# A three-stage transformer layer in split float32: the order of its transfers, and where two kinds of derived blocks are made

## The reference

```python
u = x @ w_in                                  # 1024 x 1024, four groups of 256 columns
pooled = trailing mean over 2, 4, 8, 16 tokens   # one window per group
m = (einsum(pooled - u, w_group) * scale) @ w_out
h = layer_norm(ALPHA * x + m)
gate, up = split(h @ w_gu, 2)                 # d_ff = 2816
out = layer_norm(ALPHA * h + (silu(gate) * up) @ w_down)   # meta tokens dropped
```

## Time and profile before

| | before |
|---|---|
| median of three runs | 1836.06 us |
| the profiled execution | 1835.27 us, span 1833.5 us |
| granted clock, mean | 0.968 |
| PE busy | 1692.6 us (92%), 7400 matmuls |
| DVE, ACT, POOL busy | 53%, 32%, 32% |
| DMA | 307.75 MB, mean 168 GB/s |
| PE idle and what ended it | DVE split 41.7 us, ACT acc 31.8 us, DMA nat 11.8 us, DVE acc 10.5 us |

### The profile page before, as it was taken

How to read it: one execution, slowest core, us unless ns; L and a number is a source line. 1 busy time by engine, 2 the same in 40 slices (tenths; PEclk the granted TensorE clock), 3 DMA queues, 4 the chain that set the end, 5 groups by cost and what they waited for, 6 DMA issues and landing times.

```text
span 1833.5 us, 18920 instructions
## 1 busy us (share of the span) xinstructions
PE 1692.6 (92%) x7400; PEld 1390.8 (76%) x7400; DVE 975.0 (53%) x1055; ACT 580.2 (32%) x790; POOL 586.1 (32%) x361
## 2 busy tenths in 40 slices
PE   7997876997789999999986999999999899999997
PEld 5886665876568877788875888888888788888786
DVE  6557447683675333344444554444553444458757
ACT  5232212332433333333343333333332433342220
POOL 0004323043233233343322666566652000142001
PEclk9999898998989999999997999999999999999999
DMA  8434866647625344342244445545458544555532
GB/s 327 179 115 165 284 238 222 243 143 245 247 97 162 103 137 127 116 132 69 92 145 154 151 136 157 180 134 156 131 186 265 186 142 154 186 178 202 192 131 100
DMA packets 189704, 307.75 MB, mean 168 GB/s; under 512 B 7728, under 2 KB 137904, under 8 KB 178096
## 3 DMA queue, kind: packets, MB, share of 16 engines
q1 hardware_dynamic: 189616, 306.55, 49.6%
HBM read 218.96 MB, written 87.56 MB: 167 GB/s over the span
## 4 chain that ended last, share of the span: by engine, by line
PE 69%; DMA 11%; DVE 6%; POOL 6%; issue 4%; SPq 2%; ACT 2%; ACTq 0%; DVEq 0%; POOLq 0%
PE acc L913 35%; PE acc L942 13%; PE turn L913 6%; PE turn L942 5%; PE acc L780 5%; PE acc L764 4%; DMA raw<-fold_dram 2%; POOL dt_t L618 2%; DMA dt_raw<-w_down 2%; DMA raw<-w_in 1%; POOL ss_mix L618 1%; DMA fs<-hf_dram 1%; DVE fa L1364 1%; SPq L375 1%; DVE split L1231 1%
## 5 line engine op out<-in xcount | busy, mean ns | idle before, releaser
L913 PE MATMUL acc<-fa,wf 128*128 128x512 f32 x3168 | 739.9, 394 | 43.7 <-ACT acc L1159 31.8
L913 PEld LDWEIGHTS acc<-fa,wf 128*128 128x128 f32 x3168 | 600.1, 190 | 171.3 <-DVE wf L1370 25.5
L942 PE MATMUL acc<-dw,da 128*128 128x512 f32 x1386 | 317.9, 391 | 7.8 <-DVE da L1437 6.1
L942 PEld LDWEIGHTS acc<-dw,da 128*128 128x128 f32 x1386 | 260.9, 189 | 63.6 <-DVE da L1437 7.0
L1370 DVE TENSOR_TENSOR wf<-wt,wf 128x512 fp32r<-128x512 f32 x132 | 122.4, 929 | 206.0 <-ACT wf L1072 205.8
L1370 DVE TENSOR_TENSOR wf<-wr,wf 128x512 fp32r<-128x512 f32 x176 | 169.9, 973 | 83.1 <-ACT wf L1072 82.6
L780 PE MATMUL acc<-split,act_sb 128*128 128x512 f32 x768 | 185.9, 404 | 27.4 <-DVE split L1231 16.1
L764 PE MATMUL acc<-mov,split 128*128 128x512 f32 x768 | 184.9, 401 | 28.3 <-DVE split L1231 25.6
L780 PEld LDWEIGHTS acc<-split,act_sb 128*128 128x128 f32 x768 | 149.7, 196 | 62.7 <-DVE split L1231 13.5
L764 PEld LDWEIGHTS acc<-mov,split 128*128 128x128 f32 x768 | 147.7, 194 | 61.6 <-issue 26.5
L618 POOL TENSOR_TENSOR wt<-wr,wt 128x512 f32<-128x512 f32 x88 | 127.6, 1450 | 171.1 <-DVE wf L1370 171.0
(11 more groups left out here) (94 smaller groups left out, 1329.4 us busy)
## 6 DMA issues: line engine op xcount, KB each, us to landing
wr<-w_gu SPq DMA_DIRECT2D x44, 1024.0 KB, 5.0
dar<-af_dram SPq DMA_DIRECT2D x56, 704.0 KB, 4.1
af_dram<-g SPq DMA_DIRECT2D x33, 512.0 KB, 3.3
raw<-w_in SPq DMA_DIRECT2D x16, 1024.0 KB, 9.4
raw<-fold_dram SPq DMA_DIRECT2D x16, 1024.0 KB, 9.1
fs<-hf_dram SPq DMA_DIRECT2D x14, 1024.0 KB, 4.9
dt_raw<-w_down SPq DMA_DIRECT2D x11, 1024.0 KB, 7.6
wt_dram<-dt_t SPq DMA_DIRECT2D x11, 1024.0 KB, 5.2
```

The costliest lines, as they stand in the source:

```text
L913: mm = nc.tensor.matmul(dst, wf[:, slot, a, k, :], fa[i][:, v, k, :], start=i < 2 and k == 0 and n3 == 0, stop=k == KC - 1 and n3 == 2, sk ...
L942: mm = nc.tensor.matmul(down_bank(k), da[k % 3][:, v, p, :], dw[:, slot, a, :], start=p == 0 and n3 == 0, stop=p == JF - 1 and n3 == 2)
```

## The change

**T forms.** The steps stand by a list, `TF_AT`: three beside block 0's last chunks, six beside `c_in(1, 2)` to `c_mix(1, 3)`, and two (with a last store) beside `c_in(2, 2)` to `c_mix(2, 0)`. In `mixer_block`, `load_x` now stands ahead of the step. POOL takes three forms ahead of `rstd_of(0)`, six ahead of `rstd_of(1)`.

**Turned h.** Pair 0 is turned in the last chunk of block 2, pairs 1 to 3 in `c_in(3, 0)` to `c_in(3, 2)`. They have their own landing buffer, `nat_mix`. `st_mix` is one buffer instead of two. POOL makes pair 0's sums ahead of `rstd_of(2)`. Pairs 4 to 7 are turned one in three units (5 and 6, 8 and 9, 11 and 12, 14 and 15). ACT's `take_turn` waits for `st_stored` and for `ss_made` of the pair before, no more for the landing of its sums.

**Forms.** `hf_dram` is laid out so that a pair is stored in two DMAs (768 KB and 1 MB) with runs of 2 KB and loaded in runs of 2 KB. `fa[i]` becomes `[P, 2, TT, KC, P]`: the moving operand of a product, 512 columns long, now lies in four pieces of 512 B, 2 KB apart. `fs` has four buffers for the exchange: four forms are loaded at unit 17, and the seven splits are spread over units 21 and 22 (`NEW_FORM_AT`).

**Others.** In block 3, `store_h(2, 1..3)` and `load_z(3)` go behind `load_form(1)`, just ahead of the last chunk's load. The last `store_a` and `store_s` go behind the first `load_da` of the down stage's loop.

```diff
             def store_pair(pi):
-                half, cols = pi // TT, slice(pi % TT * P, pi % TT * P + P)
-                forms = hf_dram[half].rearrange("f p k t -> p f k t")
+                half, j = pi // TT, pi % TT
+                forms = hf_dram[half].rearrange("f j p n -> j p f n")[j]
                 sp.wait_ge(turn_taken, 4 * pi + 4)
-                for f, blk in ((0, 1), (3, 2), (6, 3)):
-                    sp.dma_start(forms[:, f, :, cols], st[:, blk]).then_inc(stored, 16)
+                sp.dma_start(forms[:, 0:3, :], st_of(pi)[:, 1:4].rearrange("p f k t -> p f (k t)")).then_inc(st_stored, 16)
                 sp.wait_ge(ss_made, 4 * pi + 4)
-                for f, blk in ((1, 0), (2, 1), (4, 2), (5, 3)):
-                    sp.dma_start(forms[:, f, :, cols], ss[:, blk]).then_inc(stored, 16)
+                sp.dma_start(forms[:, 3:NP, :], ss_of(pi).rearrange("p f k t -> p f (k t)")).then_inc(ss_stored, 16)
...
+            TF_AT = [(0, 5), (0, 6), (0, 7), (1, 2), (1, 3), (1, 4), (1, 5), (1, 6), (1, 7), (2, 2), (2, 3), (2, 4)]
...
-            load_chunk(c_in(LAST, 0), 0, w_in[0])
-            load_chunk(c_in(LAST, 1), 1, w_in[1])
             load_pair(0)
-            load_chunk(c_in(LAST, 2), 0, w_in[2])
+            for i in range(3):
+                load_chunk(c_in(LAST, i), i % 2, w_in[i])
             load_pair(1)
             store_pair(0)
...
-            for j in range(1, TT):
-                store_h(LAST - 1, j)
-            load_z(LAST)
             load_chunk(c_mix(LAST, 2), 0, fold_dram[2])
             store_pair(3)
             load_form(0)
             load_form(1)
+            for j in range(1, TT):
+                store_h(LAST - 1, j)
+            load_z(LAST)
             load_chunk(c_mix(LAST, 3), 1, fold_dram[3])
...
+        NEW_FORM_AT = [(HALF_UNITS - 1, place) for place in range(3, 7)] + [(HALF_UNITS, place) for place in range(3)]
...
-                if k == 0:
-                    if pi < TT and pi >= 2:
-                        act.wait_ge(pair_stored[pi % 2], 112 * (pi // 2))
-                    elif pi > TT:
-                        act.wait_ge(pair_stored[(pi - 1) % 2], 112 * ((pi - 1) // 2 + 1))
...
+                if k == 0 and pi:
+                    act.wait_ge(st_stored, 16 * pi)
+                    act.wait_ge(ss_made, 4 * pi)
...
-                        mm = nc.tensor.matmul(dst, wf[:, slot, a, k, :], fa[i][:, v, k, :],
+                        mm = nc.tensor.matmul(dst, wf[:, slot, a, k, :], fa[i][:, v, :, k, :],
```

More of the change, by code:

```diff
@@ L1 @@
+import functools
 import math
@@ L268, in st_of, with nat_of, fs_uses, fs_holder @@
         def st_of(pi):
-            return st_mix[pi % 2] if pi < 4 else st_gu
+            return st_mix if pi < 4 else st_gu
+        def nat_of(pi):
+            return nat_mix if pi < 4 else nat
+        HF_OF = (0, 3, 4, 1, 5, 6, 2)
+        FS_SLOT = (0, 1, 0, 1, 0, 1, 0, 0, 1, 2, 3, 0, 1, 2)
+        def fs_uses(q):
+            return FS_SLOT[:q].count(FS_SLOT[q])
+        def fs_holder(q):
+            return max((r for r in range(q) if FS_SLOT[r] == FS_SLOT[q]), default=None)
         def ss_of(pi):
@@ L379, in load_form @@
                 if i == 0:
[L380 to L384, removed]
+                    sp.wait_ge(st_stored, 16 * TT * (half + 1))
+                    sp.wait_ge(ss_stored, 16 * TT * (half + 1))
+                if fs_holder(q) is not None:
+                    sp.wait_ge(fa_lo, fs_holder(q) + 1)
+                sp.dma_start(fs[FS_SLOT[q]].rearrange("p j k t -> p j (k t)"),
+                             hf_dram[half, HF_OF[i]].rearrange("j p n -> p j n")).then_inc(fs_landed[FS_SLOT[q]], 16)
             def load_unit(n):
@@ L770, in hidden, with outward @@
                         between(m)
-            def outward(c, slot, half, k0, kn, first, final, bank_is_free):
+            def outward(c, slot, half, k0, kn, first, final, bank_is_free, between=None):
                 chunk_is_split(c)
@@ L783, in outward @@
                                                   stop=final and k == kn - 1 and n3 == 2)
-                    if final and j < TT - 1:
-                        mm.then_inc(out_done, 1)
-                mm.then_inc(chunk_done, 1)
+                    if j < TT - 1:
+                        if final:
+                            mm.then_inc(out_done, 1)
+                    else:
+                        mm.then_inc(chunk_done, 1)
+                    if between is not None:
+                        between(j)
             def fold_pair_free(q):
@@ L1101, in mixer_block @@
                         x_hi(b + 1, i)
+                        if b == LAST - 1 and i == PAIRS - 1:
+                            for k in range(KC):
+                                take_turn(0, k)
                     elif i == 1:
@@ L1509, in _ @@
                         down_w_lo(v)
-                if n == HALF_UNITS - 1:
-                    for q in range(NP + 3, 2 * NP):
-                        form_lo(q)
             dve.wait_ge(prod_done, NP * UNITS)
```

161 lines of the change are left out of this document (88 added, 73 removed).

## The result

Four runs of the changed kernel gave 1760.46 to 1765.40 us, median 1760.84; the kernel before gave 1835.07 beside them. The ratio is 0.960 (95% interval 0.958 to 0.962). The forecast was 1727 with a range of 1708 to 1758: right in sign, 34 us too low, and the measured time lies 2.8 us above the range. The profiled execution took 1760.91 us, with a span of 1759.1 and a mean granted clock of 0.984 (before 0.968).

A forecast was written before the change was run, and what follows sets the result against it. PE was taken as full at full clock for most of the span, losing time to waits in four places. Gains of 27.5 + 18.7 + 24.2 + 17.7 + 18.8 + 2.5 = 109.4 us off 1835.27 gave 1725.9, forecast 1727, range 1708 to 1758.

The forecast's parts named there:

- what stays of the waits in blocks 1 and 2: Mixer blocks 1 and 2: waits of 6.7 and 1.5 us stay; gains of 27.5 and 18.7 us.
- The first wait of the rest: Block 1: PE waits some 2.2 us for DVE's split of the third chunk, behind the first pooling ending at 157.8.
- Block 3: Mixer block 3, turning pairs 1 to 3: 101.0 us, a gain of 24.2 us.
- The wait for the rows: Block 3: PE's wait of 4.97 us for DVE, whose row adds stood behind the late form 0, goes.
- Pairs 4 to 7: Units 5 to 15: three units per pair and a wait for POOL alone remove all 17.7 us lost.
- The exchange: Units 21 and 22: forms waiting in buffers gain 18.8 us; 4 us of wait for DVE's list stays.
- The down stage's start: Start of down stage: weight block goes out about 2 us earlier, gain 2.5 us (0 to 5).
- The moving operand in four pieces: Products' matmuls: taken to cost nothing, since the pieces are 128 elements long.
- Rival 1: Blocks 1 to 3: the queue still sets the pace, +25 us, 1752; chance 0.18.
- Rival 2: Waits left in the forecast are met by the splits' and loads' spread, some 15 us fewer, 1712; chance 0.12.
- Rival 3: Exchange and units still wait for ACT and DVE: exchange 10 us instead of 4, +15 in all, 1742; chance 0.09.
- Rival 4: Units 0 to 43: the moving operand in pieces slows every product, 1936 at a quarter of a matmul; chance 0.03.

The follow-up runs named there:

- both causes taken out: Changed kernel with x loaded behind the row stores and z, and POOL's sums of T forms 1 to 10 over 8 columns: 1730.98 us, ratio 0.944.
- the short sums: Changed kernel with POOL's sums of T forms 1 to 10 made over 8 of 512 columns, transfers kept: 1739.23 us, ratio 0.949.
- the last kernel: Changed kernel with T forms beside units 5 to 15 and new orders at exchange, down stage, block 3 and unit 0: 1705.44 us, ratio 0.930.

## Why the prediction was right in sign and 34 us off

**The step that failed: what stays of the waits in blocks 1 and 2.** The prediction gave them 94.1 and 90.7 us, as clean blocks plus 6.7 and 1.5 of waits; they took 109.2 and 96.5, 20.9 us more. The clean part was right (87.4 and 89.2 forecast, 87.04 and 88.84 measured with both causes taken out). The waits were counted along the queue, and for the T forms' steps that count was good: the chunks' waits went, and with the old places they return, 29.5 us. The first wait of the rest was also right, mechanism and size: 2.2 us for DVE behind the first pooling, and PE waits 2.14 at 160.49. Behind it the prediction gave DVE no further loss in block 1 and 1.5 us in block 2. What was left out is what DVE does beside POOL. After the change POOL makes six forms in block 1 and two in block 2, and there DVE's list has no room left: 21.6 us by the short sums, of which SP's shorter steps may have given a part. In the trace of before the pooling itself did not meet POOL: DVE had done a chunk's pooling before the next form reached POOL (159.28, 172.36, 188.24 us), and the group of its sums read as with the short sums:

```profile
L1264 DVE TENSOR_TENSOR sums<-sums 128x1024 f32<-128x1024 f32 x6 | 7.4, 1225 | 0.2
```

But other operations did meet it, and so the price stood in that trace. At the start of block 1 POOL makes its first form from 143.37 to 151.35 us, and the rows' normalisation beside it takes 2.2 to 2.3 us for each operation, where it takes 1.28 with POOL idle:

```profile
143.43 2.31 DVE L1308 SCALAR_TENSOR_TENSOR z<-z,rstd,gb 128x1024 f32<-128x1024 f32 x1 [0.92 <-POOL rstd L622]
145.66 2.31 DVE L1303 SCALAR_TENSOR_TENSOR z<-z,mv,gb 128x1024 f32<-128x1024 f32 x1
148.00 2.20 DVE L1308 SCALAR_TENSOR_TENSOR z<-z,rstd,gb 128x1024 f32<-128x1024 f32 x1
```

A split beside the third form takes 3.29 (176.73) instead of 2.29, and the splits' mean in the earlier trace rows, 2413 ns, is above the quiet one too. The first wait was forecast rightly because its end of the pooling, 157.8, was taken from this trace with the slowed operations in it, which the prediction does not say, so its size is partly luck; the waits after it had no such allowance. And x: its load was never followed in its new place in the queue. It waits for a split on DVE that comes at 198.68, and h, z and a chunk stand behind it: 9.5 us. Both taken out, the time is 1731, within the forecast's own range of 1717 to 1738.

Of the slowed operations the Trainium skill has the rule ("SBUF — State Buffer", Who interferes with whom): a VectorE instruction with two SBUF inputs contends with a GpSimd instruction that reads SBUF, and so does one in a two-port mode. The trace agrees: sums and splits with two SBUF inputs, and the copies of 32 columns with one, take 1.0 to 1.1 us more when they are caught; in which mode the copies ran, no trace here shows. The rule speaks against this change. The prediction thought of the slowing in two places only, at the exchange ("more if POOL slows DVE") and for POOL's sums in block 3 ("if the sums take twice as long"), and not in blocks 1 and 2, where it cost most.

**Block 3**: 101.0 forecast, 105.2 measured. Pair 3's wait was forecast at about 4 and is 4.21. The wait for the rows, forecast to go, is 2.83 with 0.76 behind it; those two are most of the 4.2. The order of POOL (pair 0's sums ahead of rstd) cost nothing that shows.

**Pairs 4 to 7**: 17.7 forecast. From the second product of unit 1 to that of unit 22 the time fell by 17.0 us (424.62 to 407.58, from 529.89 and 486.67 on). The sum was right and half of its reason wrong: not the three units. With the new stores, making ACT wait for both stores again costs 9.4; the other 7.6 are what is left for the stores in two DMAs of 2 KB runs, if the two simply add. The old layout with the new, shorter wait wasn't tried.

**The exchange**: 18.8 forecast, 14.0 measured. From the second product of unit 22 to that of unit 23 it took 27.75 us (894.25 to 922.00) for a clean 19.04, so 8.7 are lost and not 4. The mechanism was right (DVE's list of seven splits, then the add), the size not: of the seven splits, four are met by an operation of POOL, one of them taking 2.68 and three 3.35 to 3.39 us instead of 2.29. That is 3.6 us of the 4.3 between the 2.4 us of wait that the count gave and the 6.74 measured.

**The down stage's start**: 2.5 forecast, 0 measured. The stores were moved behind one load, but still stand ahead of the weights' load, which goes out 26.6 us after the stage's start, as before (26.1). Behind that load, the stores let 4.3 us go.

**The moving operand in four pieces**: nothing forecast, nothing measured: 1325 matmuls in 300 us before and after. The sentence of the Trainium skill ("Advanced Engine Details and Errata", PSUM Cachelines) that a non-contiguous access pattern slows matmuls significantly stands under PSUM; read for any operand, it does not hold here, for this one in SBUF, in pieces of 128 elements.

**The rivals.** Rival 1 came nearest in number (1752), and mostly by luck: it had the steps of the T forms set the pace, and at the three waits of blocks 1 and 2 for DVE's list the chunks were there 7.7 us and more ahead. The part of it that is true is the queue's order behind x, 9.5 us, which it did not name. Rival 2's 1712 supposed that waits would be met by spread; the waits of blocks 1 and 2 all stayed until an edit took their cause away. Rival 3 had the exchange's size right (8.7 against its 10) and was wrong on the units. Rival 4 is refuted.

**The terms**, for the profiled executions: the forecast gain was 109.4 us and the measured one 74.4 (1835.27 less 1760.91), 35.0 less. Of these, 21.0 are in blocks 1 and 2, 4.2 in block 3, 4.8 at the exchange, 2.5 at the down stage and 0.7 in pairs. Unit 0 adds 1.8, where the prediction had nothing: from the end of block 3 to the second product of unit 1 it takes 39.3 us instead of 37.5, with waits of 2.53 and 12.49 where 1.41, 11.76 and 0.17 stood. That makes 35.0. The medians are 33.8 apart, because the forecast of 1727 has 0.8 us more in it for the median of before, and is rounded.

## What to carry to other kernels

When a schedule is counted to be just in time, price the elementwise operations at what they take beside their new neighbour on the other engine: look in the trace of before for any operation of that engine with the neighbour busy, since even another operation than yours shows the price (here 2.31 us for 1.28), and take it into the sum or the range. When a transfer is moved on an in-order queue, ask first what it waits for itself and then who stands behind it; a wait of one DMA is a wait of all that follow. Work that only has to be done some time belongs beside the stage whose engines have slack, here the units, not where three engines and the queue are already in step.

## What the runs showed of the hardware

- Many elementwise operations on DVE take 1.0 to 1.1 us longer beside POOL's sums, nearly independent of their size: 1.27 instead of 0.18 us for 128x32, 2.2 instead of 1.22 for 128x1024, 3.38 instead of 2.29 for 128x2048. The smallest suffer most in proportion.
- The slowing goes both ways: POOL's sums of a T form (128x512) take from 1.26 up to 3.22 us in blocks 1 and 2, and 1.28 to 1.76 where they stand beside the units.
- DMA at a share of 0.85 and 304 GB/s in block 1 left no wait for PE.
- The clock was granted in full (1.00) in every stretch shown in which PE did not wait, and also in block 3 of the last kernel, with waits of up to 0.8 us. In the changed kernel it was 0.94 to 0.98 in blocks 1 to 3, with waits of up to 5 us, 0.88 in the unit of the exchange (one wait of 6.74 us), and 0.83 in unit 0 (waits of 2.53 and 12.49 us).
